# Loading the scale and shift rows of the next norm in the middle of the next stage

## What is computed

```python
x = first_block(x, ...)   # rms_norm, then conv branch and attention branch (16 heads), merged; + x; rms_norm
# second_block, two layers:
#   layer 0: mix = [nsa_attention(12 heads), memory_attention(4 heads)] @ w_out
#   layer 1: mix = [moba_attention(12 heads), memory_attention(4 heads)] @ w_out
x = layer_norm(ALPHA * x + mix, ln1_g[layer], ln1_b[layer])
x = layer_norm(ALPHA * x + conv_ffn(x), ln2_g[layer], ln2_b[layer])
```

## Time and profile before

| | us |
|---|---|
| median of 3 runs | 1023.41 (1021.62 to 1024.3) |
| the profiled execution | 1025.44 |
| its span, first to last instruction | 1023.8 |
| PE busy | 971.6, 95% of the span |
| DVE busy | 667.6, 65% |
| ACT busy | 525.9, 51% |
| POOL busy | 130.6, 13% |

### The profile page before, as it was taken

The page is one execution under the profiler, slowest core; times in us unless marked ns, Lnnn a source line. Parts: engine busy times, 40 slices in busy tenths (PEclk is TensorE's granted clock), DMA queues, the critical chain, the costliest instruction groups (busy, mean ns, idle before and its releaser), DMA issues.

```text
span 1023.8 us, 20016 instructions
## 1 busy us (share of the span) xinstructions
PE 971.6 (95%) x7018; PEld 875.7 (86%) x7018; DVE 667.6 (65%) x1204; ACT 525.9 (51%) x966; POOL 130.6 (13%) x154
## 2 busy tenths in 40 slices
PE   7999999999999888989899999998899989999995
PEld 5899999999899776757789999996888679999995
DVE  5566666665666857864876666668566576666665
ACT  5444555545444647754545555554466455555553
POOL 3000000000100402630510000005200060000001
PEclk9999999999999999989999999999999999999998
DMA  7555555556455375313365555553654345555552
GB/s 251 176 185 174 174 174 174 174 171 224 145 204 184 125 245 172 100 36 117 103 218 187 183 183 182 188 177 124 222 167 157 124 135 199 185 182 184 186 183 79
DMA packets 48226, 172.89 MB, mean 169 GB/s; under 512 B 6031, under 2 KB 6479, under 8 KB 48060
## 3 DMA queue, kind: packets, MB, share of 16 engines
q1 hardware_dynamic: 44732, 159.78, 45.9%
q0 software_dynamic: 3456, 12.61, 4.0%
HBM read 171.29 MB, written 1.07 MB: 168 GB/s over the span
## 4 chain that ended last, share of the span: by engine, by line
PE 78%; DVE 9%; ACT 6%; DMA 4%; issue 2%; POOL 1%; SPq 0%; POOLq 0%; DVEq 0%; ACTq 0%
PE bank L1318 17%; PE bank L1320 17%; PE bank L1319 17%; PE ysum L1366 6%; PE ysum L1368 6%; PE ysum L1367 6%; DVE sb_wl L806 4%; DMA sb_raw<-in_stream 4%; ACT sb_wh L417 2%; PE bank L1397 2%; PE ysum L1410 1%; PE ysum L1404 1%; ACT sb_xh L442 1%; DVE sb_z L852 1%; ACT sb_pr L462 1%
## 5 line engine op out<-in xcount | busy, mean ns | idle before, releaser
L806 DVE TENSOR_TENSOR sb_wl<-sb_raw,sb_wh 128x1024 fp32r<-128x1024 f32 x300 | 388.7, 1299 | 181.8 <-ACT sb_wh L417 180.7
L1318 PE MATMUL bank<-sb_xh,sb_wh 128*128 128x256 f32 x1360 | 389.4, 286 | 3.9 <-DVE sb_t_a L1230 2.4
L1320 PE MATMUL bank<-sb_xh,sb_wl 128*128 128x256 f32 x1360 | 385.8, 284 | 0.0
L1319 PE MATMUL bank<-sb_xl,sb_wh 128*128 128x256 f32 x1360 | 385.7, 284 | 0.0
L417 ACT ACTIVATE sb_wh<-sb_raw 128x1024 fp32r<-128x1024 f32 x300 | 314.1, 1052 | 126.1 <-PE ysum L1368 52.9
L1318 PEld LDWEIGHTS bank<-sb_xh,sb_wh 128*128 128x128 f32 x1360 | 261.5, 192 | 14.3 <-issue 4.8
L1319 PEld LDWEIGHTS bank<-sb_xl,sb_wh 128*128 128x128 f32 x1360 | 261.7, 192 | 1.8
L1320 PEld LDWEIGHTS bank<-sb_xh,sb_wl 128*128 128x128 f32 x1360 | 261.8, 193 | 0.0
L1366 PE MATMUL ysum<-sb_wh,sb_mh 128*128 128x512 f32 x208 | 82.6, 397 | 1.6 <-DVE sb_ml L816 1.6
L1367 PE MATMUL ysum<-sb_wl,sb_mh 128*128 128x512 f32 x208 | 82.2, 395 | 0.0
L1368 PE MATMUL ysum<-sb_wh,sb_ml 128*128 128x512 f32 x208 | 82.2, 395 | 0.0
(11 more groups left out here) (264 smaller groups left out, 1442.4 us busy)
## 6 DMA issues: line engine op xcount, KB each, us to landing
sb_raw<-in_stream SPq DMA_DIRECT2D x300, 512.0 KB, 3.3
sb_bias<-rel_rows POOLq DMA_DIRECT2D x12, 384.0 KB, 3.7
sb_bias<-in_alibi POOLq DMA_DIRECT2D x8, 256.0 KB, 3.2
sb_gb<-in_ln_g POOLq DMA_DIRECT2D x4, 512.0 KB, 4.1
sb_gb<-in_ln_b POOLq DMA_DIRECT2D x4, 512.0 KB, 6.8
sb_x_tok<-in_x SPq DMA_DIRECT2D x2, 512.0 KB, 3.8
sb_memf<-in_mem_t POOLq DMA_DIRECT2D x1, 1024.0 KB, 5.7
out<-sb_x_tok SPq DMA_DIRECT2D x2, 512.0 KB, 2.6
```

Of the source, the lines that this page charges most:

```text
L806: dve.tensor_tensor(wl[slot][:, :, :], raw[slot][:, :, :], wh[slot][:, :, :].bitcast(F32), ALU.subtract).then_inc(split_l, 1)
L1318: pe.matmul(out, wh[slot][:, k, :], mov_h(k), start=k == 0, stop=False)
L1319: pe.matmul(out, wh[slot][:, k, :], mov_l(k), start=False, stop=False)
L1320: last = pe.matmul(out, wl[slot][:, k, :], mov_h(k), start=False, stop=k == KT - 1)
```

## The change

`load_gb` is called at other places. The load of the final norm's scale of the first block comes after POOL has stored the position rows, ahead of the loop over head pairs, and not at once after norm n0. The rows for n2 are loaded in the NSA loop at pair 2, behind the position bias of pair 3, and not at the end of `tail` of n1. The rows for n3, n4 and n5 wait in addition for `used`: 18 blocks into the first feed forward stage, the end of pair 2's k block (block 217) in the MoBA stage, and 18 blocks into the second feed forward stage. In the MoBA stage, POOL's issues of the position bias of pairs 0 and 1 are put ahead of the load of the rows, and those of pairs 2 to 5 stay behind it.

```diff
             low_odd("n0")
-            load_gb(a["final_g"], None)
...
             pool.dma_start(rel_rows, relf[:, :]).then_inc(rel_out, 16)
+            load_gb(a["final_g"], None)
             with pool.Fori(1, PAIRS1) as i:
...
             tail("n1", False)
-            norm_wait(pool, "n1", "x", 2)
-            load_gb(a["ln1_g_2"][0], a["ln1_b_2"][0])
             for i in range(PAIRS2):
                 if i + 1 < PAIRS2:
                     relative("p3", i + 1, 12)
+                if i == 2:
+                    norm_wait(pool, "n1", "x", 2)
+                    load_gb(a["ln1_g_2"][0], a["ln1_b_2"][0])
...
-            for nm, g, b, row in (("n2", "ln2_g_2", "ln2_b_2", 0),
-                                  ("n3", "ln1_g_2", "ln1_b_2", 1),
-                                  ("n4", "ln2_g_2", "ln2_b_2", 1)):
+            for nm, g, b, row, block in (("n2", "ln2_g_2", "ln2_b_2", 0, B_FFN0 + 18),
+                                         ("n3", "ln1_g_2", "ln1_b_2", 1, B_QK + 6),
+                                         ("n4", "ln2_g_2", "ln2_b_2", 1, B_FFN1 + 18)):
                 for t in range(NT):
                     rstd(nm, t, EPS_LN)
                 low_odd(nm)
                 tail(nm, True)
+                if nm == "n3":
+                    pool.wait_ge(S["p3", "max"], 12 * PAIRS2)
+                    for i in range(2):
+                        relative("p5", i, 4)
                 norm_wait(pool, nm, "x", 2)
+                pool.wait_ge(used, block)
                 load_gb(a[g][row], a[b][row])
                 if nm == "n3":
-                    pool.wait_ge(S["p3", "max"], 12 * PAIRS2)
-                    for i in range(PAIRS2):
+                    for i in range(2, PAIRS2):
                         relative("p5", i, 4)
```

## The result

The changed kernel takes 1027.47 us (median of 20 runs, 1024.79 to 1030.27), the kernel before 1025.62 in the runs beside it (median of 20). The ratio is 1.0021, with a 95% interval from 1.0011 to 1.0031: slower by 2.1 us, between 1.1 and 3.2. The forecast was 0.6 us faster, with a loss and a gain that nearly cancel. The place is right, the sign is not. (The runs shown ahead of the prediction lay at the low end of what the kernel before does, so the difference counts, not the 1022.8.)

A forecast was written before the change was run, and what follows sets the result against it. The prediction took PE to bound the kernel, busy 971.6 of 1023.8 us. 8.8 us gained less 8.2 lost made it 0.6 us faster, 1022.8 us on the median, range 1018.6 to 1027.8.

The forecast's parts named there:

- The MoBA wait: MoBA pair 2: bias queued behind k block wait and rows, PE stands 6.5 us; cost 8.2 us with clock.
- The clock term: Behind the wait at MoBA pair 2: PE's clock halved for 3.4 us, costing 1.7 us.
- Rival B: MoBA pair 2: bias does not really queue behind the rows; net gain 4.3 us, 1019.1; chance 0.19.
- Rival C: MoBA pair 2: bias lands after 9.4 us, 12.1 us lost against 8.8 gained, 1026.7; chance 0.08.
- The first MoBA pair: Start of the MoBA stage: 2.5 us of gap and 1.2 of clock regained, 3.7 us gained.
- The feed forward stages: Both feed forward stages: 0.3 and 0.8 us gained at their starts, cost 0 each in their middle.
- The NSA stage: NSA projections: PE's 2.77 us gap closes and most of the clock returns, 2.8 + 1.2 = 4.0 us gained.
- rival D: Removal gives back less, NSA shift lost to load waits: 4.3 us gained against 8.2 lost, 1027.3; chance 0.13.
- The load of norm n1's scale: Near 19 to 55 us PE is busy at the load's old and new place; nothing either way.
- A: Whole kernel: gains and losses both real, cancel to within 3.1 us; 1022.8, range 1020.4 to 1026.4; chance 0.60.

The follow-up runs named there:

- idle_filled: The changed kernel, with 24 matmuls of zeros on PE while it waits for pair 2's probabilities; ratio 1.0003 to the kernel before.
- n3_alone: The kernel before with only the MoBA part of the change; ratio 1.0049, 5.0 us slower.
- one_row_ahead: The changed kernel, with pair 2's position bias issued between the scale row and the shift row; ratio 1.0015 to the kernel before.
- wait_kept: The changed kernel, with pair 2's bias issued behind the k block wait but ahead of both rows; ratio 0.9985 to the kernel before, 1.5 us faster.
- all_but_n3: The changed kernel without its MoBA part; ratio 0.9975 to the kernel before, 2.6 us faster.
- ffn_alone: The kernel before with only the two feed forward parts of the change; ratio 0.9976, 2.5 us faster.
- n3_alone_bias_first: The kernel before with only the MoBA part, pair 2's bias issued ahead of the wait and rows; ratio 0.9969, 3.2 us faster.
- bias_first: The changed kernel, with pair 2's bias issued ahead of the k block wait and rows; ratio 0.9913 to the kernel before, run again 0.9936.

## Why the prediction was wrong, step by step

**The MoBA wait: mechanism right, price 0.8 us too low.** The bias behind the wait for the k block, behind the rows, 7.2 us to landing, all on PE: forecast 6.5 us of idle, measured 6.75. The clock term was mis-sized: I took 1.7 us from the gaps of 2.8 and 3.0 us in the kernel before, as half of a stretch of 3.4. Here 4.5 us of half clock lay behind the wait, and 9.0 - 6.75 = 2.2 us were lost there, of which idle_filled wins back 1.6. The other kernels with the wait bear this out: with 3.8, 5.9 and 6.3 us of half clock behind it (n3_alone, one_row_ahead, wait_kept), what is lost beyond the idle time is 1.9, 2.8 and 3.0 us, each time about half. So 9.0 in place of 8.2. Rival B, that the bias does not queue, is out: landing moves with what is ahead of it, 5.7, 6.1 and 7.2 us for none, one and two rows. Rival C's 9.4 us to landing did not come either. What the prediction had no term for is that POOL's three transfers first wait for SP's block loads: no packet of POOL's queue is moved until 747.2 us, 2.7 us behind the first issue. The 7.2 us to landing hold that wait, so their agreement with the forecast, which put it together from other parts, is in part luck.

**The first MoBA pair: right.** Forecast 3.7 us. The MoBA stage takes 119.87 before and 116.43 to 116.55 with the order mended, 3.4 gained net of all. The split into 2.5 for the gap and 1.2 for the clock holds too: in all_but_n3, which keeps the load at its old place, PE waited 2.92 us and the granted clock stayed at 1.00 behind it. Its MoBA stage takes 118.79 us, 1.1 less than before and 2.3 more than with the load moved.

**The feed forward stages: right.** Forecast 0.3 and 0.8, measured 0.4 and 1.0. That the 6.37 us piece of the chain was worth only 0.3 is confirmed. In the middle of the stage nothing is lost, though a block load issued 3 us after the rows takes 5.6 us to land: in the changed kernel ACT's splits start at 560.90 and 563.61, which is 562.51 and 565.22 less 1.61 us, and by the same 1.61 us the splits of ten blocks ahead of these and ten behind them are earlier.

**The NSA stage: this term was mis-sized most.** I took the gap of 2.77 us and most of the half clock behind it, 4.0 us in all, and wrote that the shift is carried on. In the kernels with the load at its old place the stage n1 to NSA pair 1 takes 61.04, 60.52, 60.67 and 63.56 us (before, ffn_alone, n3_alone_bias_first, n3_alone). With the load moved it takes 58.5 to 59.5 in eight of ten executions (58.54, 58.65, 58.82, 58.91, 58.96, 58.96, 59.19 and, in all_but_n3, 59.51). In the other two, the changed kernel and wait_kept, it took 62.37 and 60.97: there a block load landed late with no rows in flight, PE waited 2.8 and 2.0 us, and the clock was down at 384 us. The same happened in n3_alone, with the load at its old place, so it is not the change's doing. The medians are 60.9 and, over all ten, 59.0, so some 2.0 us are gained. The gap does close: ACT splits the block behind it, number 112, 2.0 to 2.7 us earlier, counted from the split of block 104. But that is all. Behind it the stage waits for its block loads, as rival D had it for this one term: from 366 to 398 us ACT waited 11.4 us for them in bias_first, 9.6 in the kernel before. So the 1.2 us of clock did not come back as time, and part of the 2.8 was given back as well. A stretch of half clock at 354 us, which five of the ten have and five have not, does not show in the stage's time either.

**The load of norm n1's scale: right.** Forecast nothing. Norm n1 starts at a median of 337.6 us in the nine executions with that load moved, and at 337.8 in the five with it at its old place.

**The sum, made again from stages:** 2.0 + 0.4 + 3.4 + 1.0 = 6.8 us gained. The three runs with the order mended gave 8.9, 6.6 and 6.1, on average 7.2. Less 9.0 us lost is 2.2 us slower; measured 2.1 and, the second time, 1.3. So the forecast failed by two terms of its sum, both on the same side: 8.8 gained should have been 7 (the NSA stage), 8.2 lost should have been 9.0 (the clock behind the wait). The case was A, and the range held. But A had 0.6 us faster and D 3.9 us slower, and the result lies about midway.

What stays open: why ffn_alone came out 1.1 us better (2.5 against 1.4) and all_but_n3 0.8 us worse (2.6 against 3.4) than these stages say. Both lie within their intervals of 1.5 us either way, and the profiles show one reason why such intervals are wide here: the NSA pairs, which the change does not slow, took 88.9, 90.5, 91.9 or 93.5 us, according to how much half clock fell in them. The table's differences are themselves read from one execution of each kernel. And where in the NSA stage the time goes that PE no longer idles is read from waits, not tested by a run.

## What to carry to other kernels

When a load is put behind a wait, everything that its engine issues after it waits too: look for a transfer there that is needed soon after the event that the wait names. Here it was a single buffered bias needed 1.7 us after the event, and moving that one issue ahead was worth 8 to 11 us. A piece of the chain of waits is no gain in itself (6.37 us of it were worth 0.4); read PE's idle time at its end, and ask what limits the stage next.

## What the runs showed of the hardware

The stretches of half clock between the first stage and norm n5 are 3.4 or 6.8 us long in all 14 traces. Behind 4.1, 5.2, 6.7, 6.75 and 6.9 us of idle time it was 6.8 each time, and filling the wait with matmuls of zeros removed it. Behind the waits of 2.7 to 3.2 us in the NSA stage and at the first MoBA pair it was 3.4 seven times, but 6.8 in the changed kernel (behind 2.82 us, the second row of the windows above), and in all_but_n3 (behind 2.92 us) there was none. So the length of the wait alone does not tell what follows. In the NSA pairs half clock also came without a longer wait, in some executions and not in others of the same code. The same stretch in the view by windows, in the changed kernel's second execution:

```profile
444.10:450.90 6.80, 6.80 (x34) 3.76 (x33) 2.44 (x8) 0.94 (x5) 4.25 (x8) 0.50 0.01 2
```

And in bias_first's second:

```profile
444.10:450.90 6.80, 6.34 (x49) 3.89 (x48) 3.92 (x12) 3.71 (x16) 4.25 (x8) 1.00 0.01 2
```

34 matmuls against 49 in the same 6.8 us, with PE busy in both. A stretch of 3.4 us costs the pairs 1.6 us and one of 6.8 us costs 3.0, as much as the whole effect measured here.

Loads on two queues are not always served side by side. In wait_kept only packets of SP's queue were moved from 745.1 to 747.8 us, while the bias issued at 745.07 stood on POOL's. The other way round, this is all that the DMA view of the kernel before has from 720.6 to 722.9 us:

```profile
q0 software_dynamic: 136, 0.53, 82.2%
```

That is POOL's queue, with the rows issued at 719.56. The block loads that SP had issued at 720.5 and 721.65 got nothing until then, and landed after 7.4 and 9.1 us. In both cases the queue that was already being served went on first. This is what pushed the stream back at this place of the kernel before, and it delayed the bias in the changed one. On one queue, transfers overlap in part: in wait_kept 59 packets of the rows start before the last one of the bias ahead of them is done.
